# Beginning a projection with half of its features, and giving two low parts to Pool

## The reference, cut to what matters

```python
x = ...                                   # (1, 256, 1024) float32
# layer 0 of a stack of several
shift, scale, gate = split(silu(c) @ ada_w[0] + ada_b[0], 3)
h = rmsnorm(x, norm_g[0]) * (1 + scale) + shift
proj = h @ a_in_w[0]                      # 1024 x (4 * 1024 + 16)
qkv = silu(causal_depthwise_conv(proj[..., :3072], conv_w))   # 4 taps
z, b, a = proj[..., 3072:4096], proj[..., 4096:4104], proj[..., 4104:]
# q, k normed by l2norm; then a gated delta rule in chunks, a gate with silu(z), out_w
```

## Time and profile before

| | us |
|---|---|
| median of 3 runs | 1082.59 |
| lowest, highest | 1080.59, 1085.85 |
| the profiled execution | 1079.84 |
| its span in the profile | 1078.0 |
| TensorE busy in the span | 1018.3 (94%) |
| VectorE, ScalarE, Pool busy | 699.0, 599.6, 128.2 |

### The profile page before, as it was taken

One profiled execution on the slowest core, in us unless ns is written; L12 is line 12 of the kernel. 1 busy time (PEld: TensorE's weight loads), 2 busy tenths in 40 slices (PEclk: granted clock), 3 DMA queues, 4 the chain that ended last, 5 costly groups with the idle time before them and its releaser, 6 DMA issues. The chain is left out here.

```text
span 1078.0 us, 16874 instructions
## 1 busy us (share of the span) xinstructions
PE 1018.3 (94%) x6978; PEld 918.7 (85%) x6978; DVE 699.0 (65%) x1010; ACT 599.6 (56%) x910; POOL 128.2 (12%) x119
## 2 busy tenths in 40 slices
PE   2699999999899999899999899999999989999997
PEld 2699989898898888779888798999879869889995
DVE  5789775966866676777565665455557876555454
ACT  4455577664564666555576654434456976434443
POOL 1010028460200122621000010000000100000000
PEclk9899999999999999999999999999999999999999
DMA  9776435543487632235333365555544355555540
GB/s 351 234 206 179 156 118 177 176 157 91 126 259 253 222 119 78 79 118 191 122 118 118 93 219 196 179 179 189 194 157 157 118 158 193 173 185 192 195 157 39
DMA packets 120428, 178.40 MB, mean 165 GB/s; under 512 B 5189, under 2 KB 80099, under 8 KB 120353
## 3 DMA queue, kind: packets, MB, share of 16 engines
q1 hardware_dynamic: 118816, 172.40, 49.3%
q0 software_dynamic: 1120, 2.97, 0.9%
q10 hardware_dynamic: 416, 1.97, 0.5%
HBM read 176.27 MB, written 1.05 MB: 164 GB/s over the span
## 5 line engine op out<-in xcount | busy, mean ns | idle before, releaser
L1410 DVE TENSOR_TENSOR sb_w_lo<-sb_raw,sb_w_hi 128x2048 fp32r<-128x2048 f32 (+1 forms) x143 | 320.9, 2245 | 215.3 <-ACT sb_w_hi L734 215.0
L734 ACT ACTIVATE sb_w_hi<-sb_raw 128x2048 fp32r<-128x2048 f32 x140 | 265.8, 1901 | 130.8 <-PE G L2241 111.9
L2239 PE MATMUL X<-sb_hT_hi,sb_w_hi 128*128 128x256 f32 x960 | 273.7, 285 | 5.4 <-DVE sb_w_lo L1410 2.7
L2240 PE MATMUL X<-sb_hT_lo,sb_w_hi 128*128 128x256 f32 x960 | 271.4, 283 | 0.0
L2241 PE MATMUL X<-sb_hT_hi,sb_w_lo 128*128 128x256 f32 x960 | 271.2, 283 | 0.0
L2239 PEld LDWEIGHTS X<-sb_hT_hi,sb_w_hi 128*128 128x128 f32 x960 | 183.4, 191 | 8.7 <-DVE sb_w_lo L1410 4.4
L2240 PEld LDWEIGHTS X<-sb_hT_lo,sb_w_hi 128*128 128x128 f32 x960 | 183.6, 191 | 0.6
L2241 PEld LDWEIGHTS X<-sb_hT_hi,sb_w_lo 128*128 128x128 f32 x960 | 183.5, 191 | 0.0
L2239 PE MATMUL G<-sb_w_hi,sb_uT_hi 128*128 128x512 f32 x304 | 121.5, 400 | 4.8 <-DVE sb_uT_lo L2179 4.8
L2241 PE MATMUL G<-sb_w_hi,sb_uT_lo 128*128 128x512 f32 x304 | 120.7, 397 | 0.0
L2240 PE MATMUL G<-sb_w_lo,sb_uT_hi 128*128 128x512 f32 x304 | 120.6, 397 | 0.0
(11 more groups left out here) (467 smaller groups left out, 1729.5 us busy)
## 6 DMA issues: line engine op xcount, KB each, us to landing
sb_raw<-in_mlp_w SPq DMA_DIRECT2D x64, 1024.0 KB, 5.2
sb_raw<-in_ada_w SPq DMA_DIRECT2D x24, 1024.0 KB, 5.3
sb_raw<-in_a_in_w SPq DMA_DIRECT2D x16, 1024.0 KB, 5.8
sb_raw<-in_b_in_w SPq DMA_DIRECT2D x16, 1024.0 KB, 5.5
sb_raw<-in_sb_w_qkv SPq DMA_DIRECT2D x12, 1024.0 KB, 5.2
sb_raw<-in_rg_w_in SPq DMA_DIRECT2D x8, 1024.0 KB, 5.3
sb_raw<-in_a_out_w SPq DMA_DIRECT2D x4, 1024.0 KB, 5.0
sb_raw<-in_b_out_w SPq DMA_DIRECT2D x4, 1024.0 KB, 5.0
```

The source lines that it names most:

```text
L734: nc.scalar.activation(split_tile(w_hi, m)[:, 0:nk * w], raw[b % RAW_SLOTS][:, 0:nk * w], ACT.Copy).then_inc(S["w_hi"], 1)
L1410: ins = nc.vector.tensor_tensor(split_tile(w_lo, m)[:, at], raw[b % RAW_SLOTS][:, at], split_tile(w_hi, m)[:, at].bitcast(F32), ALU.subtract)
L2239: dt32(out, lh, rh, start=first, stop=False, skip_group_check=shared)
L2240: dt32(out, lh, rl, start=False, stop=False, skip_group_check=shared)
```

## The change

Eight things change together. (1) The block list interleaves: four ada blocks for features 0 to 511, then the weights of these features for the first six feature blocks (three blocks of 4 chunks x 512 columns), then the same for features 512 to 1023, then a_ba, then feature blocks 6 to 11 as before. (2) Modulation, high and low parts and products run by halves; the six first feature blocks accumulate in six psum banks (`half_block`, two feature blocks in each weight block). (3) x is loaded first from SP's queue, and only the first 258 columns of the constants early. (4) Two weight blocks (m = 1 and 2) are loaded into zs and osb, which are free then, and Pool makes their low parts. (5) The statistics of x and half of the transposes go ahead of the end of the Toeplitz work. (6) The sixteen few columns come behind the first six feature blocks. (7) Until a_z there are three split slots instead of two; `QKV_SPLIT` says which block is split in which round of the conv. (8) ScalarE makes the first of the four conv taps. The third split slot is counted, so later slot numbers shift. The diff, cut to its core:

```diff
-    for n in range(4):
-        ada(0, n)
     a_in = I["a_in_w"][0]
+    for half in range(2):
+        for n in (half, 2 + half):
+            ada(0, n)
+        for j in range(3):
+            rows(f"a_qkv{half}", a_in, slice(j * 512, (j + 1) * 512), 4 * half, 4)
     feature_major("a_ba", a_in, 4 * AW, 2 * AH)
-    for n in range(12):
+    for n in range(6, 12):
         feature_major("a_qkv", a_in, n * 256)
...
+                with ExitStack() as conv_stage:
+                    w_hi.append(sb("w_hi_conv", [P, BLK], F32R, conv_stage))
+                    w_lo.append(sb("w_lo_conv", [P, BLK], F32R, conv_stage))
...
-        TR_BANK = {"h0": TB + G[2:4], "h1": G}
+        TR_BANK = {"h0": TB + TB, "h1": G}
+        QKV_BANK = G + X
+        TOEP_BANK = G + [X[1]] + G[0:3]
...
+        few_m, m_z0 = first_mm["a_ba"], first_mm["a_z"]
         for m in range(len(mm_raw)):
-            if m < three[0]:
-                slot[m] = m % SPLIT_SLOTS
+            if m < m_z0:
+                slot[m] = -1 if m == few_m else (m if m < few_m else m - 1) % 3
+            elif m < three[0]:
+                slot[m] = (m + 1) % SPLIT_SLOTS
...
+        apart = {mm_raw[1]: (zs[:, :, :].rearrange("p m d -> p (m d)"), "params_in", 32),
+                 mm_raw[2]: (osb[:, :, :].rearrange("p m d -> p (m d)"), "x_in", 32)}
+        ring = [b for b in range(len(blocks)) if b not in apart]
...
+        def qkv_m(f):
+            return first_mm["a_qkv1"] + f // 2 if f < 6 else first_mm["a_qkv"] + f - 6
+
+        QKV_SPLIT = {1: 7, 2: 8, 3: 9, 5: 10, 6: 11, 7: 12, 8: 13, 9: 14}
...
+            sp.dma_start(xres[:, :, :], I["x"].rearrange("b (m p) d -> p (b m) d", p=P)).then_inc(S["x_in"], 16)
             for b, (kind, _, src, nk, n) in enumerate(blocks):
-                if b >= RAW_SLOTS:
-
-                    old = b - RAW_SLOTS
+                if b == mm_raw[few_m]:
+                    sp.wait_ge(S["consts_in"], 16)
+                    sp.dma_start(consts[:, EARLY_CONST:], I["consts"][:, EARLY_CONST:]).then_inc(S["consts_in"], 16)
+                if b in apart:
+                    sp.wait_ge(raw_in(b), loaded(b) - 16)
...
+            for m in (1, 2):
+                b = mm_raw[m]
+                pool.wait_ge(S["w_hi"], m + 1)
+                pool.wait_ge(S["w_split"], m)
+                nc.gpsimd.tensor_tensor(split_tile(w_lo, m)[:, :], raw_of(b)[:, :], split_tile(w_hi, m)[:, :].bitcast(F32),
+                                        ALU.subtract).then_inc(S["w_split"], 1)
...
+            act.dma_start(consts[:, 0:EARLY_CONST], I["consts"][:, 0:EARLY_CONST]).then_inc(S["consts_in"], 16)
...
+            def h0_hi(half):
+
+                act.wait_ge(S["mod"], half + 1)
+                transposed_hi("h0", shifted=0, groups=range(2 * half, 2 * half + 2))
+                if half == 1:
+                    act.wait_ge(S["hT_lo"], 4 * TR["h0"] + 2)
+                for c in range(2):
+                    k = 4 * half + 2 + c
+                    ins = nc.scalar.activation(tpair[1][:, c, :], TR_BANK["h0"][2 * half + 1][:, c * T:(c + 1) * T], ACT.Identity,
+                                               scale=mod_scale[0][:, k:k + 1], bias=mod_shift[0][:, k:k + 1])
+                    ins.then_inc(S["h0_whole"], 1)
+
...
             split_hi(0)
-            transposed_hi("h0", shifted=0, groups=range(2))
-            split_hi(1)
-            transposed_hi("h0", shifted=0, groups=range(2, 4))
-            act.wait_ge(S["hT_lo"], 4 * TR["h0"] + 2)
-            for c in range(2):
-                ins = nc.scalar.activation(tpair[1][:, c, :], TR_BANK["h0"][3][:, c * T:(c + 1) * T], ACT.Identity,
-                                           scale=mod_scale[0][:, 6 + c:7 + c], bias=mod_shift[0][:, 6 + c:7 + c])
-                ins.then_inc(S["h0_whole"], 1)
-
-            split_hi(2)
-            few_copy("a_ba", 2 * AH)
+            h0_hi(0)
+            for m in range(1, 4):
+                split_hi(m)
+            h0_hi(1)
+            for m in range(4, 7):
+                split_hi(m)
...
             for f in range(12):
-                m = first_mm["a_qkv"] + f
-                act.wait_ge(S["w_used"], m + 1)
+                act.wait_ge(S["w_used"], qkv_m(f) + 1)
                 if f >= 2:
                     act.wait_ge(S["conv"], f - 1)
-                nc.scalar.activation(xpad[f % 2][:, :, CONV - 1:T + CONV - 1], X[f % 2][:, :].rearrange("p (c t) -> p c t", c=2),
+                nc.scalar.activation(xpad[f % 2][:, :, CONV - 1:T + CONV - 1],
+                                     QKV_BANK[f % 6][:, :].rearrange("p (c t) -> p c t", c=2),
                                      ACT.Copy).then_inc(S["fm_out"], 1)
-                split_hi(m + 2)
-                if f == 1:
+                act.wait_ge(S["fm_out"], f + 1)
+                if f >= 2:
+                    act.wait_ge(S["conv_silu"], f - 1)
+                for c in range(2):
+                    ins = nc.scalar.activation(cacc[f % 2][:, c, :], xpad[f % 2][:, c, 0:T], ACT.Copy,
+                                               scale=taps[:, 0, 2 * f + c:2 * f + c + 1])
+                    if c == 0:
+                        ch.mark(ins)
+                ins.then_inc(S["tap0"], 1)
+                if f in QKV_SPLIT:
+                    split_hi(QKV_SPLIT[f])
+                if f == 4:
+                    few_copy("a_ba", 2 * AH)
+                if f == 6:
                     decay_exps()
                 if f >= 1:
                     conv_silu(f - 1)
...
-            dve.wait_ge(S["csil"], 1)
-            ada_sum()
-
...
-            for _i in range(7):
-                ada_sum()
-            split_lo(0)
-            modulation(0)
-            shifted_lo("h0", 0, range(2))
-            split_lo(1, 0)
-            shifted_lo("h0", 0, range(2, 3))
-            split_lo(1, 1)
-            dve.wait_ge(S["h0_whole"], 2)
-            dve.wait_ge(S["hT_hi"], 4 * TR["h0"] + 4)
-            nc.vector.tensor_tensor(hT_lo[:, 6:8, :], tpair[1][:, :, :], hT_hi[:, 6:8, :].bitcast(F32), ALU.subtract)\
-                .then_inc(S["hT_lo"], 1)
-            split_lo(2)
-
-            ba = G[1][:, 0:32].rearrange("p (m n) -> p m n", m=MT)
+            dve.wait_ge(S["csil"], 1)
+            for half in range(2):
+                for _i in range(4):
+                    ada_sum()
+                modulation(0, half + 1, (X[0], TB[1])[half], 4 * half, 4)
+                shifted_lo("h0", 0, range(2 * half, 2 * half + 1))
+                split_lo(3 * half, 0)
+                dve.wait_ge(S["h0_whole"], 2 * half + 2)
+                dve.wait_ge(S["hT_hi"], 4 * TR["h0"] + 2 * half + 2)
+                gs_ = slice(4 * half + 2, 4 * half + 4)
+                nc.vector.tensor_tensor(hT_lo[:, gs_, :], tpair[1][:, :, :], hT_hi[:, gs_, :].bitcast(F32), ALU.subtract)\
+                    .then_inc(S["hT_lo"], 1)
+                split_lo(3 * half, 1)
+                for m in () if half == 0 else (4, 5, few_m):
+                    split_lo(m)
...
                 if f == 11:
                     norm_factors()
-                dve.wait_ge(S["fm_out"], f + 1)
-                if f >= 2:
-                    dve.wait_ge(S["conv_silu"], f - 1)
-                for k in range(CONV):
+                dve.wait_ge(S["tap0"], f + 1)
+                for k in range(1, CONV):
                     for c in range(2):
...
+                if f in QKV_SPLIT:
+                    split_lo(QKV_SPLIT[f])
+                if f == 6:
                     decay_last()
-                if f == 4:
...
+            def h0_transposes(groups):
+
+                for m in range(MT):
+                    pe.wait_ge(S["xn_ready"], XN["h0"] - 1 + m)
+                    for g in groups:
+                        for c in range(2):
+                            k = 2 * g + c
+                            ins = transpose(TR_BANK["h0"][g][:, c * T + m * P:c * T + (m + 1) * P],
+                                            xn[:, m, k * P:(k + 1) * P], ident)
+                        if m == MT - 1:
+                            ins.then_inc(S["tr_done"], 1)
+
             for g in range(8):
-                if g >= 4:
-                    pe.wait_ge(S["toep_out"], g - 3)
+                if g == 5:
+                    pe.wait_ge(S["consts_in"], 16)
+                    h0_transposes(range(2))
+                if g >= 5:
...
+            def first_columns(half):
+
+                bank = (X[0], TB[1])[half]
+                for i in range(2):
+                    pe.wait_ge(S["ada_used"], 4 * half + 2 * i + 2)
+                    for c in range(8 * i + 4 * half, 8 * i + 4 * half + 4):
+                        ins = dt32(bank[:, c:c + 1], ada_acc[:, c * P:(c + 1) * P], one_col, start=True, stop=True)
+                ins.then_inc(S["ada_cols"], 1)
+
+            first_columns(0)
             pe.wait_ge(S["toep_out"], 9)
...
+            def half_block(half, j):
+
+                m = 3 * half + j
```

(84 more changed lines are left out.)

125 lines of the change are left out of this document (63 added, 62 removed).

## The result

| | before | after |
|---|---|---|
| median, us | 1082.66 (12 runs) | 1084.36 (12 runs) |
| lowest, highest | 1080.59, 1085.85 | 1083.43, 1086.68 |
| the profiled execution | 1079.84 | 1084.2 |
| its span | 1078.0 | 1082.4 |

The ratio is 1.0018, with a 95% interval of 1.0010 to 1.0026. The change costs 1.7 us where I had forecast a gain of 2.1. The value of 1084.36 is inside my range (1074.5 to 1085.0), and within half a per cent of before, but on the other side of before than the forecast, beyond the interval. Between the two profiled executions the loss is larger, 4.4 us; I come back to the difference.

What follows compares the result with a forecast made beforehand. TensorE, busy 94% of the span, bounds the kernel. 16.8 - 9.1 - 1.4 - 0.35 - 0.5 - 4.2 = +1.25, with the tail's 0.9 a gain of 2.1 us: median 1080.5, 8-in-10 range 1074.5 to 1085.

Steps and rivals of the forecast that it cites:

- The start: First half of the projection: dense products start at 27.0 instead of 43.88, a gain of 16.8 us.
- only four columns wait, which saves half of 1.45: Between the end of the ada sums and ScalarE's first high part: 1.4 instead of 2.1 us.
- Pool's instructions and the hold: Pool's two low parts take 4.5 us each and hold VectorE's sums until 49.8; the hold costs 3.3 us.
- The gap: Between the halves TensorE stands from 46.1 until the second half's products start at 55.2: a loss of 9.1 us.
- The slow starts: At both halves' starts the clock has fallen to 0.50, costing 1.4 us each.
- My sign: Profile check for slow starts: the granted clock reads 0.50 at the starts of both halves.
- The wait behind f = 10: End of the projection: TensorE waits for ScalarE's split, SiLU and square of kT before the norms, a loss of 4.2 us.
- rival (1): Pool's hold does not bind, the clock stays up, or both: gain 5.4 to 8.1 us, 1074.5 to 1077; chance 0.32.
- The last copy: End of the projection: the last block's copy comes near 123.2.
- The tail: Behind the last block, the next step's product comes 11.05 instead of 12.0 us after it: a gain of 0.9 us.
- Later stages shift as a whole: Stages after the projection keep their order and shift as a whole.
- The distance between trace and median: The median stays 2.75 us above the profiled execution, so 1077.7 profiled becomes 1080.5 as median.

Runs made afterwards that it cites:

- The two fills: Against e4_both: five spare products in the first gap, 1071.8 us; or zero-adding spare products in the gap between the halves, 1073.02 us.
- the wait filled: Changed kernel plus 36 spare TensorE products between feature block f=10 and the squared norms: 1082.27 us, ratio 1.0002 to the kernel before.
- The square first: Changed kernel with ScalarE's split of m=14 moved behind the SiLU and square of kT in round f=9: 1076.62 us, ratio 0.9955 to the kernel before.
- e4_both: Changed kernel with the square of kT ahead of that split and both of Pool's low parts made by VectorE: 1073.95 us, ratio 0.9928 to the kernel before.

## Why the prediction was wrong

- **The start, right in kind, 1.9 short.** First start 28.87 for 27.0; sums 22.4 for 21.6, as the fourth ada block is waited for (timeline of VectorE after: idle 0.60 before its sum at 19.25). The other us is the step "only four columns wait, which saves half of 1.45". The eight instructions in the earlier trace rows were already four columns: after, 16 columns are four rows of eight, so a one-column float32 product shows as two instructions, and there was nothing to halve. (The 2.7 us for x's megabyte went by 390 GB/s, which the earlier trace rows do not show, they have 412; the busy times of before read 390 from 22 to 24 us, and the first sum came at 9.83 for 9.6.)
- **Pool's instructions and the hold, right.** 4.58 and 4.61 for 4.5, sums' end 51.2 for 49.8, which is the late start handed on. Without Pool the second start is 2.7 earlier in one trace and 1.7 in the other, for my 3.3. The Trainium skill's 4497 ns ("GPSIMD Engine Reference", section 3.1) was as near.
- **The gap, right.** 8.3 us (48.65 to 56.96) for 9.1. Second start 56.96 for 55.2.
- **The slow starts, right in kind.** I took 1.4 for each. After, about 20 products ran at 0.213 us instead of 0.119 at the first start, which is 1.9, and about 16 at the second, 1.5; in other traces of these starts it was 12 to 25 products, 1.1 to 2.3. The two fills gave 1.6 each at the end of the stage. My sign, a granted clock of 0.50 in both starts, came only at the second.
- **The wait behind f = 10, right at 4.38 for 4.2, and here is the step that failed.** I wrote "-4.2" for a pause of four us of an engine that I had just charged for two slow starts after pauses of that kind. The cost behind it is the missing term, which I had put at nothing without a reason: the wait filled shows 4.1, from the 12.79 us between the norms and the last copy down to 8.72. The error was one of consistency: in rival (1) I had even asked whether the clock falls at a start "long after" an idle stretch, and did not ask it of the stretch that my own change made.
- **The last copy adds up:** 123.2 + 1.8 (second start) + 0.2 (wait) + 4.1 (clock) = 129.3; it was 129.43. So close a fit is this one trace's: the same slow stretch costs 3.0 to 4.4 from trace to trace.
- **The tail, right in kind.** From the copy to the next product after, 140.17, it is 10.7 us for my 11.05 and 11.95 before: a gain of 1.2 for 0.9.
- **"Later stages shift as a whole", nearly.** Between the two traces the distance is 3.7 us until 435, 4.35 from 475 on. In between the clock fell once after and not before, without any change in that code (after):

```profile
443.00:446.00 3.00, 3.00 (x15) 2.98 (x15) 2.99 (x3) 2.70 (x10) 3.00 (x2) 0.50 0.00 0
```

- **The whole adds up too.** The forecast gain of 2.1, less 1.8, 0.2 and 4.1, with 0.3 more from the tail and 0.65 less from this later fall, is a loss of 4.35; between the two traces it is 4.36.
- **The distance between trace and median, open.** By the traces the change loses 4.4, by the medians 1.7. I carried over that before's profiled execution is 2.75 below its median; after's is 0.2 below. That step failed too, and in my favour: with 0.2 the same mistakes would have given a forecast of 1077.9. What the last section shows makes the fall of the clock in later pauses a candidate for this spread. No trace shows the other executions, so it is argued, not shown.

## What to carry to other kernels

A pause of the bound engine that a change opens costs its length and can cost as much again in the slow pace behind it, here 4.4 and, from trace to trace, 3.0 to 4.4 us. Ask for both in every new wait, and first see whether the order of a queue can close it: moving one weight split behind the square was worth 7.7 us. Work given to a second engine is not free if the two exclude each other: two low parts cost VectorE 4.4 us when it made them and 8.2 when Pool did.

## What the runs showed that I had not expected

**The granted clock's record is not the pace.** At the first start of the changed kernel it reads 1.00 in all traces, while the products ran at 0.213 us, as they do at 0.50 elsewhere, and spare products ahead of them brought 0.119. Before that start TensorE had made small Toeplitz products and columns, these already at half pace (eight instructions in 1.86 us at 22.42, in 0.95 at 48.65), and then stood for 4.6 us. The Trainium skill says as much ("TensorE: Matmul & The Clock Gate", Part 1: "the default state is throttled, and activity releases the throttle"), and this case's pace agrees while its clock record does not. At a start, count matmuls.

**Later pauses give or take 1 to 3 us with their place.** The square first has its last copy 8.1 us earlier than after, but ends 6.0 earlier. One place is near 885, where TensorE waits for VectorE's low part of h. The timeline of TensorE and the busy times of the square first:

```profile
886.08 0.36 PE L2299 MATMUL X<-sb_hT_hi,sb_w_hi 128*128 128x256 f32 x1 [1.83 <-DVE sb_hT_lo L1823]
```

```profile
888.00:890.00 2.00, 2.00 (x11) 2.00 (x11) 0.00 (x0) 0.00 (x0) 0.00 (x0) 0.50 0.71 291
```

The same row after:

```profile
893.59 0.36 PE L2298 MATMUL X<-sb_hT_hi,sb_w_hi 128*128 128x256 f32 x1 [0.27 <-DVE sb_hT_lo L1822]
```

The wait was 1.8 instead of 0.3 there, and the clock fell. VectorE and ScalarE keep the same distances in both traces (the low part begins 4.14 us after ScalarE's weight split); TensorE's transposes ahead of it stand at 880.42 and 889.47, so that TensorE was 1.5 us further ahead of VectorE in the first. Why is not followed further back. The same wait of 1.80 to 1.82 us, and a clock that falls to between 0.50 and 0.57 behind it, are in four more traces (the wait filled, without Pool, the second gap filled, the first gap filled in the changed kernel). The other traces wait 0.42 us or less there, e4_both not at all, and their clock stays at 1.00. For an edit that is worth a few us, the trace of its stage says more than the median of five runs.
